# Moving the SBUF tiles of a PE-bound two-layer trunk by 32 bytes

## The reference

```python
for i in range(DEPTH):                       # DEPTH = 2
    hn = rms_norm(h, norm_mix_g[i])
    h = h + (fox_mixer(hn, ...) if i % 2 == 0 else gla_mixer(hn, ...))
    h = h + sqrelu_mlp(rms_norm(h, norm_mlp_g[i]), mlp_w_up[i], mlp_w_down[i])
return rms_norm(h, norm_final_g)
# sqrelu_mlp(h, w_up, w_down) = square(relu(h @ w_up)) @ w_down
```

## The kernel before

| tile | start | beyond a multiple of 2048 | beyond a multiple of 64 |
|---|---|---|---|
| `ident` (moving operand of the transposes) | 16512 | 128 | 0 |
| `w_stage` | 18464 | 32 | 32 |
| `w_hi` | 51232 | 32 | 32 |
| `w_lo` | 84000 | 32 | 32 |
| `hT_hi`, `hT_lo` | 116768, 133152 | 32 | 32 |
| `h`, `gates_split` | 149536, 165920 | 32 | 32 |
| inner blocks begin (`hn`, `vo`, `u_raw`, `o_all`) | 168992 | 1056 | 32 |
| `u_hi3` | 185376 | 1056 | 32 |
| `u_lo3` | 206880 | 32 | 32 |

## Time and profile before

### The profile page before, as it was taken

The page is one execution under the profiler, slowest core; times in us unless marked ns, Lnnn a source line. Parts: engine busy times, 40 slices in busy tenths (PEclk is TensorE's granted clock), DMA queues, the critical chain, the costliest instruction groups (busy, mean ns, idle before and its releaser), DMA issues.

```text
span 1159.6 us, 14739 instructions
## 1 busy us (share of the span) xinstructions
PE 1147.6 (99%) x5617; PEld 960.1 (83%) x5617; DVE 795.8 (69%) x1008; ACT 563.3 (49%) x793; POOL 39.5 (3%) x88
## 2 busy tenths in 40 slices
PE   9999999999999999999999999999999999999997
PEld 7788888888888888888878998987888888888886
DVE  5647777645874866858867775593478478387586
ACT  5446667526534535535556333353454354353454
POOL 2000000000000000000020001010000000000001
PEclk9999999999999999999999999999999999999999
DMA  9347665432153071251242320205122414215202
GB/s 291 75 85 155 131 143 154 124 122 73 37 183 108 4 237 49 63 191 37 84 146 66 110 79 32 73 6 177 35 75 82 173 37 150 104 36 181 87 30 82
DMA packets 116250, 119.07 MB, mean 103 GB/s; under 512 B 39010, under 2 KB 84098, under 8 KB 116196
## 3 DMA queue, kind: packets, MB, share of 16 engines
q1 hardware_dynamic: 113328, 117.26, 34.1%
q10 hardware_dynamic: 2868, 1.07, 0.4%
HBM read 103.57 MB, written 2.10 MB: 91 GB/s over the span
## 4 chain that ended last, share of the span: by engine, by line
PE 94%; DVE 2%; issue 1%; ACT 1%; POOL 0%; SPq 0%; DMA 0%; POOLq 0%; DVEq 0%; ACTq 0%
PE bank L1100 10%; PE bank L1104 10%; PE bank L1103 10%; PE bank L1265 9%; PE bank L1270 9%; PE bank L1269 9%; PE bank L1113 5%; PE bank L1117 5%; PE bank L1116 5%; PE bank L1369 2%; PE bank L1373 2%; PE bank L1372 2%; PE bank L1417 2%; PE bank L1404 1%; PE bank L1490 1%
## 5 line engine op out<-in xcount | busy, mean ns | idle before, releaser
L662 ACT ACTIVATE w_hi<-w_stage 128x2048 fp32r<-128x2048 f32 x80 | 152.1, 1914 | 148.8 <-PE bank L1265 92.4
L1756 DVE TENSOR_TENSOR w_lo<-w_stage,w_hi 128x2048 fp32r<-128x2048 f32 x88 | 200.6, 2288 | 32.4 <-ACT w_hi L662 11.9
L1100 PE MATMUL bank<-hT_lo,w_hi 128*128 128x512 f32 x512 | 199.8, 390 | 0.0
L1104 PE MATMUL bank<-hT_hi,w_lo 128*128 128x512 f32 x512 | 199.3, 389 | 0.0
L1103 PE MATMUL bank<-hT_hi,w_hi 128*128 128x512 f32 x512 | 199.2, 389 | 0.0
L1265 PE MATMUL bank<-w_lo,u_hi 128*128 128x512 f32 x336 | 131.7, 392 | 0.0
L1269 PE MATMUL bank<-w_hi,u_hi 128*128 128x512 f32 x336 | 130.8, 389 | 0.0
L1270 PE MATMUL bank<-w_hi,u_lo 128*128 128x512 f32 x336 | 130.8, 389 | 0.0
L1100 PEld LDWEIGHTS bank<-hT_lo,w_hi 128*128 128x128 f32 x512 | 96.1, 188 | 20.5 <-DVE hT_lo L1830 0.5
L1104 PEld LDWEIGHTS bank<-hT_hi,w_lo 128*128 128x128 f32 x512 | 96.1, 188 | 20.1
L1103 PEld LDWEIGHTS bank<-hT_hi,w_hi 128*128 128x128 f32 x512 | 96.1, 188 | 19.6
(11 more groups left out here) (254 smaller groups left out, 2026.3 us busy)
## 6 DMA issues: line engine op xcount, KB each, us to landing
w_stage<-in_mlp_w_up_dram SPq DMA_DIRECT2D x32, 1024.0 KB, 5.5
w_stage<-in_mlp_w_down_dram SPq DMA_DIRECT2D x32, 1024.0 KB, 6.1
w_stage<-in_fox_w_in_dram SPq DMA_DIRECT2D x36, 256.0 KB, 5.0
w_stage<-in_gla_w_in_dram SPq DMA_DIRECT2D x8, 1024.0 KB, 5.3
qa<-qk_hi SPq DMA_DIRECT2D x32, 128.0 KB
w_stage<-in_fox_w_out_dram SPq DMA_DIRECT2D x4, 1024.0 KB, 5.6
w_stage<-in_gla_w_in_dram SPq DMA_DIRECT2D x8, 512.0 KB, 4.7
w_stage<-in_gla_w_out_dram SPq DMA_DIRECT2D x4, 1024.0 KB, 5.0
```

Source lines behind the costliest of these rows:

```text
L662: act.activation(w_hi[:, HI_SLOT[unit], :], w_stage[:, STAGE[unit], :], ACT.Copy).then_inc(w_hi_made, 1)
L1100: a = pe.matmul(out, w[0][:, k, :], x[1][:, k, :], start=(k == 0), stop=False)
L1104: a = pe.matmul(out, w[1][:, k, :], x[0][:, k, :], start=False, stop=(k == KT - 1))
L1756: dve.tensor_tensor(w_lo[:, to, :], w_stage[:, at, :], fp(w_hi[:, to, :]), ALU.subtract).then_inc(w_lo_made, 1)
```

## The change

Three tiles of 16 bytes that TensorE never reads (`through`, `oss`, `orstd`) go behind the big tiles, two of 32 bytes (`turn`, `warm`) come before them, and `orstd` is asked for with 64 bytes, of which the first 16 are used.

```diff
         columns_of = sb("columns_of", [P, 7, TB])
...
-        through = sb("through", [P, TB])
-        oss = sb("oss", [P, TB])
-        orstd = sb("orstd", [P, TB])
+        turn = sb("turn", [1, 8])[:, 0:1]
+        warm = sb("warm", [P, 8])[:, 0:1]
         w_stage = sb("w_stage", [P, SLOTS, UNIT])
...
         half_rstd = sb("half_rstd", [P, 2 * TB])[:, 0:TB]
         gn = sb("gn", [P, 8])[:, 0:2]
-        turn = sb("turn", [1, 8])[:, 0:1]
-        warm = sb("warm", [P, 8])[:, 0:1]
+        through = sb("through", [P, TB])
+        oss = sb("oss", [P, TB])
+        orstd = sb("orstd", [P, 4 * TB])[:, 0:TB]
```

## The result

The changed kernel takes 1168.72 us (1168.51 to 1168.82, four runs), the kernel before, run beside it, 1160.95. The ratio is 1.0066, 95% interval 1.0052 to 1.0080: slower by 7.8 us, where 50 us less had been forecast.

The account below looks back on a forecast made before the run. The prediction took the spacing of TensorE's matmuls as the bound: 50.7 us saved at 512 columns plus 4.8 at 256 make 55.5, less 5 for waits, 50.5, giving 1110.5 of 1160.9 us (likeliest 1111); range 1104 to 1162.

Parts of the forecast that it names:

- 13.3 ns per matmul: TensorE's full-rate matmuls: time lost beyond the columns' own, 226.7 against 213.3 ns with 512 columns, some 12.8 with 256.
- The least of 109 ns for 256 columns: TensorE's 256-column matmuls: the weight load allows no less than 109 ns, so 456 save 10.5 ns each, 4.8 us.
- a block of 128 bytes: TensorE's moving operands: a stream begun inside a block fetches one more, 17 for 2048 bytes, 544 column times or 226.7 ns.
- 11.7 ns saved per 512-column matmul: TensorE's 512-column matmuls: aligned streams go from 226.7 to 215.0 ns; 4332 of them save 50.7 us.
- 55.5 us of cure: All counted TensorE matmuls: 50.7 us from 512 columns and 4.8 from 256, before 5 us given back to waits.
- Rival A: TensorE streams: blocks of 64 bytes, only half the loss goes, 6.7 ns per matmul, 1131 us; chance 0.20.
- full cure: TensorE streams: alignment removes the extra block, 215.0 ns per 512-column matmul, likeliest time 1111 us; chance 0.42.
- the stationary one: Matmuls loading u_hi3, u_lo3, vo: these come only to multiples of 64, but the moving operands get the cure.
- Rival C: Matmuls loading u or vo: distance from w goes 1024 to 1088 bytes, 6.6 ns more each, 8 us, 1169; chance 0.06.
- distances of 0 and 1024 cost the same now: TensorE operand pairs: equal cost at these two distances, held against a slowdown from u or vo at 1088 bytes.
- Rival B: TensorE streams: the loss is a gap of the full-rate mode at any address, or the shift is harmless; 1160.9 us, chance 0.32.

Follow-up runs that it names:

- the grid: Small kernel without the computation, groups of 24 equal matmuls with stationary and moving operands at varied starts; (96,96) took 226.6 ns, (64,32) 233.1.
- e5: Changed kernel with through, oss and orstd packed into one 64-byte tile, u and vo again 1024 bytes from w: 1161.16 us, ratio 1.0000 to the kernel before.
- m2: Small kernel without the computation, operand distance 0 to 496 bytes in steps of 16, 512 and 256 columns; 512 columns took 226.7 ns at 144, 233.2 at 64.
- m3: Small kernel without the computation, with other load widths, column counts and bf16 operands; bf16 took 215.8 ns, a load of 16 columns 231.7 at distance 0.

## Why the prediction was wrong

**Right.** The kernel is bound by the distance of its matmuls: 7.3 of 7.4 us of the longer span are PE's, and its waits are 5.5 us as before. That VectorE, ScalarE, DMAs and the moved small tiles cost nothing held: VectorE is busy for 795.5 us against 795.8, ScalarE for 562.9 against 563.3, and the 1024 KB loads of `mlp_w_up` into `w_stage` land in a median of 5.2 us against 5.5, with their queue's packets taking 32.2% of the DMA engines' time against 34.1%. The 13.3 ns per matmul were read rightly for the widths looked at. At distance 0 the small kernels have 120.0, 173.3 and 226.9 ns with 256, 384 and 512 columns: 0.417 ns per column and 13.3 to 13.6 beside them. A pass of plain float32, at 0.83 ns per column, has 215.8 with 256 columns, 2.5 over 213.3. The traces give the clock as a share of full alone; that 2.4 columns per ns are one column per cycle of 2.4 GHz was the author's reading. The least of 109 ns for 256 columns, put down to the weight load, was an estimate from the earlier trace rows: 128 columns take 111.5 at D = 0, 64 and 192, and no group of 256 less than 113.4.

**The step that failed** is the hypothesis that a stream begun inside a block of 128 bytes costs one block more, and that "begun on a boundary they would be 512 and 256 columns". 17 x 32 = 544 matched and 9 x 32 = 288 matched by chance: at multiples of 2048 line 1100 keeps 226.4 ns, and in the grid (0,0) has 226.9 and (96,96) 226.6. In place of 11.7 ns saved per 512-column matmul, the runs showed nothing saved by alignment: e5 has every start aligned and every distance of before, and takes 1161.16 us against 1161.31. The whole of the 55.5 us of cure hung on it. Rival A fell with it (no distance gave 220). That full cure got 0.42 had a second fault: the match with the earlier trace rows is one coincidence and not two, since any fixed loss of 32 column times fits both rows. Nor did the range leave room for a rise: its upper end, 1162, is "nothing", and C with its 0.06 lay outside.

**The step beside it**, that `u` and `vo` need no care because they are "the stationary one", is where the 7.8 us came from: their distance from `w` went from 1024 to 1088 bytes, and the `u` matmuls from 227.8 to 233.5 ns. Weight loads and matmuls run at the same time (960.8 and 1154.9 us busy in a span of 1167.0), and how their operands lie to each other is what the change altered. In the grids no other engine is at work (from 22 to 348 us of m2 PE is busy for 326.00 of 326.00 us, ScalarE and GpSimd for 0.00), and the distance between PE's own two operands alone moves the spacing, from 226.6 to 234.3 ns in m2.

**Rival C** had the place, lines 1265 to 1270 and `vo` with line 1100 unmoved, nearly the size, 6.6 ns where `u` rose by 5.7, and the end, 1169 against 1168.72. It held 0.06. That the end fits so closely is luck: its 7.9 us for `u` and `vo` are 6.7 in the trace, and 0.8 come from slot 3, which it didn't count. What was held against it, that "distances of 0 and 1024 cost the same now", was no evidence: both are 0 modulo 256, and so is every distance in the groups that the prediction counted. Its price was borrowed from the 233 ns of the earlier trace rows, and that was luck too: by m3 a load of 16 columns costs 231.7 by itself at distance 0, so those rows need no bad distance.

**Rival B** took the 13.3 ns for the mode's own, and of a shift of both operands together that is right: it fits e5. It doesn't cover a change of distance: the D of the fine grid, all multiples of 16 bytes, differ by up to 7.7 ns.

**Still open.** These are why 0, 144 and 240 are the good distances, what the remaining 13.3 ns are that the float32r streams have and bf16 has not, and what picks one of two rhythms at 192. It is also not shown whether a matmul is slowed by its own operands' distance or by that of the load that runs beside it: in a group of the small kernel both are the same, and in the changed kernel the slot 3 matmuls are slow (230.8 ns against 228.3 before), also where the load that runs beside one is from slot 3 itself (230.9 against 226.8). What in the hardware makes the period of 256 bytes, no run shows. Nor was the better distance of the 256-column matmuls tried by itself: they share `w` and `hT` with the 512-column ones.

## What to carry to other kernels

For float32r matmuls of 512 columns with a load of 128 columns each, keep the start of the stationary operand a multiple of 256 bytes from that of the moving one (226.6 to 228.0 ns in the small kernels, mostly 232 to 234 elsewhere), and don't care for absolute alignment (e5, with every start aligned, 1161.16 us against 1161.31). Check this after every change of layout: a small tile put between two big ones shifts them against each other. For 256 columns, or for narrow loads, the runs give other good distances (116.6 ns at 224 against 120.0 at 0; with 96 columns loaded 228.3 at 64 against 229.9 at 0). A number that fits a hypothesis is worth little while the trace has no case on the other side of it; where all operands share one property, a small kernel that varies it costs less than a layout. And ask of any two tiles that one instruction pair reads what their distance is before and after, even if neither is the one that the change speaks of.

## What the hardware showed that was not expected

Single-pass float32r matmuls of 512 columns take 226.6 to 236.4 ns by the distance between their operands: 226.6 to 228.0 at multiples of 256 bytes, mostly 232 to 234 elsewhere. With bf16 it is 215.8 ns at all four distances tried, and a pass of plain float32 over 256 columns takes 215.8 at both. The effect turns round with 256 columns, 120.0 ns at distance 0 against 116.6 at 224. Its sign matters: +64 takes 233.2 to 233.5, while -64 takes 228.7 to 229.1 in most groups but 233.3 or 233.4 in three. And it carries over to neighbours: 335 matmuls whose own distance never changed went from 228.3 to 230.8 ns, standing among the matmuls of `u`.
